# Loads, ones products and conditioning steps moved in a two-block transformer kernel

## What is computed

```
def first_block(x, ...):
    h = x
    for layer in range(DEPTH):                    # DEPTH = 2
        h = hybrid_layer(h, norm_gain[layer], w_in[layer], f_bias[layer], w_branch[layer], w_out[layer])
    return rms_norm(h, final_gain)

def modulate(x, g, shift, scale):
    return rms_norm_2(x, g) * (1 + scale) + shift

# second block, layer 0, for x and for ctx:
    h   = modulate(x,   norm1_g[0], sh1,  sc1)
    h_c = modulate(ctx, norm1_g[0], csh1, csc1)
    y, y_c = even_mixer(h, ...), even_mixer(h_c, ...)     # h @ w_in first: columns v, f, u
```

## Time and profile before

| | us |
|---|---|
| median of 3 runs | 1578.64 (1578.16 to 1579.22) |
| the profiled execution, whole | 1579.09 |
| its span on the core | 1577.3 |
| PE busy | 1538.7 |
| DVE busy | 1039.6 |
| ACT busy | 756.5 |

### The profile page before, as it was taken

How to read it: one execution, slowest core, us unless ns; L and a number is a source line. 1 busy time by engine, 2 the same in 40 slices (tenths; PEclk the granted TensorE clock), 3 DMA queues, 4 the chain that set the end, 5 groups by cost and what they waited for, 6 DMA issues and landing times.

```text
span 1577.3 us, 31432 instructions
## 1 busy us (share of the span) xinstructions
PE 1538.7 (98%) x13599; PEld 1472.3 (93%) x13599; DVE 1039.6 (66%) x1347; ACT 756.5 (48%) x1132; POOL 100.7 (6%) x79
## 2 busy tenths in 40 slices
PE   5999999999999999999999999999999999989999
PEld 5999999999999999899999999999999996889999
DVE  5878767578877775554456758886345347766674
ACT  4555554465465544653355322233245327655453
POOL 0311000003010000000020000000011002000000
PEclk9999999999999999999999999999999999989999
DMA  7676454566774546512035557754335224245854
GB/s 263 217 242 221 163 178 149 183 228 208 241 241 160 188 161 211 178 64 81 28 108 174 174 180 241 243 179 143 90 116 174 90 81 102 86 134 154 234 172 136
DMA packets 312333, 260.92 MB, mean 165 GB/s; under 512 B 24066, under 2 KB 298498, under 8 KB 312068
## 3 DMA queue, kind: packets, MB, share of 16 engines
q1 hardware_dynamic: 294260, 253.52, 49.6%
q10 hardware_dynamic: 17936, 5.40, 1.6%
HBM read 257.85 MB, written 1.05 MB: 164 GB/s over the span
## 4 chain that ended last, share of the span: by engine, by line
PE 54%; issue 7%; DVE 5%; ACT 3%; DMA 0%; POOL 0%; ACTq 0%; DVEq 0%; SPq 0%; POOLq 0%
PE banks_g L1417 34%; PE banks_g L967 7%; PE banks_g L1127 5%; PE banks_g L1276 2%; DVE w_lo L2498 1%; ACT near_p L2043 1%; DVE w_lo L2200 1%; PE banks_g L956 1%; ACT w_hi L1794 1%; PE banks_g L1378 1%; PE bank_s L1450 0%; POOL bias L2128 0%; PE bank_t L1464 0%; DVE near_max L2792 0%; PE bank_t L894 0%
## 5 line engine op out<-in xcount | busy, mean ns | idle before, releaser
L1417 PE MATMUL banks_g<-h_hi,w_lo 128*128 128x256 f32 x1296 | 360.5, 278 | 1.0 <-DVE w_lo L2498 0.6
L1417 PE MATMUL banks_g<-h_lo,w_hi 128*128 128x256 f32 x1296 | 358.5, 277 | 0.0
L1417 PE MATMUL banks_g<-h_hi,w_hi 128*128 128x256 f32 x1296 | 358.5, 277 | 0.0
L2498 DVE TENSOR_TENSOR w_lo<-raw,w_hi 128x2048 fp32r<-128x2048 f32 (+1 forms) x100 | 207.6, 2076 | 100.6 <-ACT w_hi L1794 100.3
L2200 DVE TENSOR_TENSOR w_lo<-raw,w_hi 128x2048 fp32r<-128x2048 f32 x92 | 212.4, 2310 | 72.5 <-ACT w_hi L1594 72.2
L1417 PEld LDWEIGHTS banks_g<-h_hi,w_lo 128*128 128x128 f32 x1296 | 243.5, 188 | 3.0 <-issue 0.9
L1417 PEld LDWEIGHTS banks_g<-h_hi,w_hi 128*128 128x128 f32 x1296 | 243.6, 188 | 0.0
L1417 PEld LDWEIGHTS banks_g<-h_lo,w_hi 128*128 128x128 f32 x1296 | 243.3, 188 | 0.1
L967 PE MATMUL banks_g<-h_hi,w_lo 128*128 128x256 f32 x800 | 226.0, 283 | 0.3 <-DVE w_lo L2200 0.3
L967 PE MATMUL banks_g<-h_hi,w_hi 128*128 128x256 f32 x800 | 221.4, 277 | 0.0
L967 PE MATMUL banks_g<-h_lo,w_hi 128*128 128x256 f32 x800 | 221.4, 277 | 0.0
(11 more groups left out here) (414 smaller groups left out, 3277.3 us busy)
## 6 DMA issues: line engine op xcount, KB each, us to landing
raw<-w_in SPq DMA_DIRECT2D x76, 1024.0 KB, 4.8
raw<-w_up SPq DMA_DIRECT2D x88, 512.0 KB, 4.9
ada_raw<-ada_w SPq DMA_DIRECT2D x24, 1024.0 KB, 7.1
raw<-w_down SPq DMA_DIRECT2D x32, 704.0 KB, 4.3
raw<-w_branch SPq DMA_DIRECT2D x12, 1024.0 KB, 4.9
ada_raw<-ada_t SPq DMA_DIRECT2D x12, 1024.0 KB, 4.9
late_raw<-ada_t SPq DMA_DIRECT2D x12, 1024.0 KB, 5.0
raw<-qkv SPq DMA_DIRECT2D x12, 1024.0 KB, 4.9
```

The source lines that it names most:

```text
L1417: last = nc.tensor.matmul(to, w[:, c, m0:m0 + P], a[:, c, s_ * SEQ:s_ * SEQ + SEQ], start=(m, s_, c, n) == (0, 0, 0, 0), stop=(m, s_, c, n ...
L2498: nc.vector.tensor_tensor(w_lo[:, u % SLOTS, 0:n], raw[:, u % SLOTS, 0:n], w_hi[:, u % SLOTS, 0:n].bitcast(F32), ALU.subtract).then_inc(dv ...
```

## The change

The parts, by place:

1. **Start.** `vectors` leads SP's queue and `ident` goes by ACT's; x follows in two halves of its columns, and the first weight unit in two halves of 512 KB; the loads of units 0 to 3 and of the first `ada_raw` no longer wait for PE. The six constant tables go behind unit 2 in SP's queue. PE multiplies a tile of ones by itself 8 times before the transposes and 12 times after them, into a bank that unit 0 overwrites. Unit 0 starts when the first half of its weights is split and asks for the second at chunk 4. DVE makes `o_lo` straight from the banks, and copies to `x_t` after that. The squares of x are summed along its rows by ACT (two `Square` with an accumulator), in place of four ACT squares, three DVE additions and four PE products; one small product keeps the step "sumsq" in PE's count.
2. **Between the layers.** ACT's splits of the next layer's first two units follow the squares of `out` 1 and 2, not 2 and 3.
3. **End of layer 1.** ctx comes in two transfers, issued at units 40 and 41, the first behind the products "values15"; four tables of the end go from there to the end's unit 2. The norm of ctx is made after units 39 and 41 to 43, its transposes follow units 43 and 44, its modulation units 44 and 45, its splits units 44, 45 and 47. The squares of x at the end of layer 1 get tiles of their own and are summed on DVE to two tiles, so that "final sums" is 8 products instead of 16; it stands inside the ctx part of `vs` 0 ahead of chunk 6, and "spread00" inside that of `vs` 1 ahead of chunk 4. The two x parts of `vs` are one loop over chunks, which feeds each chunk to both units.

```diff
+            order.append(("ctx prep", n - 40))
...
+        if n in (43, 44):
+            order += [("ctx turn", 2 * (n - 43)), ("ctx turn", 2 * (n - 43) + 1)]
+        if n in (44, 45):
+            order += [("ctx h", 4 * (n - 44) + c) for c in range(4)]
+        order.extend(("ctx split", b) for b, at in enumerate((44, 44, 45, 47)) if n == at)
...
+        if n == 39:
+            order.append(("ctx prep", 0))
+        if n == 41:
+            order.append(("ctx prep", 1))
...
-    order = [("ctx turn", b) for b in range(4)] + [("final sums",)]
...
+    order = [("final root",), ("second root",)]
...
-            sp.dma_start(ident[:, :], ins["ident"]).then_inc(x_loaded, 16)
-            sp.dma_start(vec_in, ins["vectors"].rearrange("(a p) f -> p a f", p=P)).then_inc(x_loaded, 16)
-            sp.dma_start(x_in, ins["x"][0].rearrange("(t p) f -> p t f", p=P)).then_inc(x_loaded, 16)
+            sp.dma_start(vec_in, ins["vectors"].rearrange("(a p) f -> p a f", p=P)).then_inc(vec_loaded, 16)
+            for n in range(2):
+                sp.dma_start(x_in[:, :, n * 512:n * 512 + 512],
+                             ins["x"][0].rearrange("(t p) f -> p t f", p=P)[:, :, n * 512:n * 512 + 512]
+                             ).then_inc(x_loaded[n], 16)
...
-                    sp.wait_ge(pe_steps, pe_.at(f"unit{before}", before=u < SLOTS))
-                    sp.sem_inc(sp_passed, 1)
+                    if layer or u >= SLOTS:
+                        sp.wait_ge(pe_steps, pe_.at(f"unit{before}", before=u < SLOTS))
+                        sp.sem_inc(sp_passed, 1)
...
+                    if (layer, u) == (0, 0):
+                        sp.dma_start(dst[:, 0:KC // 2, :], src[:, 0:KC // 2, :]).then_inc(half_loaded, 16)
+                        dst, src = dst[:, KC // 2:KC, :], src[:, KC // 2:KC, :]
                     sp.dma_start(dst, src).then_inc(raw_loaded[u % SLOTS], 16)
...
+                    if u in (40, 41) and layer == DEPTH - 1:
+                        t = u - 40
+                        if t == 0:
+                            sp.wait_ge(pe_steps, pe_.at("values15"))
+                        sp.dma_start(c_in[:, t, :], ins["ctx"][0, t * P:t * P + P, :]).then_inc(ctx_loaded[t], 16)
+                    if u == (1 if layer else 2):
...
+                        if layer == 0:
+                            for dst, src in ((rope[:, :, :], ins["rope"]), (causal[:, :, :], ins["causal"]),
+                                             (upto[:, :, :], ins["upto"]), (pick[:, :], ins["pick"]),
+                                             (add_parts[:, :], ins["add_parts"]),
+                                             (fbias[:, :, :].rearrange("p l h -> p (l h)"),
+                                              ins["forget_bias"].rearrange("(o l) h -> o (l h)", o=1
+                                                                           ).to_broadcast([P, DEPTH * 8]))):
+                                sp.dma_start(dst, src).then_inc(consts_loaded, 16)
...
+                        if u == (1 if (layer, n) == (0, 0) else min(slot_n + 2, len(UNITS) - 1)):
...
+                if u == 2:
+                    sp.dma_start(w_s[:, :, :], ins["w_s"].rearrange("g p q -> p g q")).then_inc(end_loaded, 16)
...
+                    sp.dma_start(dft_c[:, :], ins["dft_c"]).then_inc(end_loaded, 16)
+                    sp.dma_start(dft_t[:, :, :, :], ins["dft_t"]).then_inc(end_loaded, 16)
...
-            pe.wait_ge(x_loaded, 16 * 3)
+            def warm(n):
+                for _ in range(n):
+                    nc.tensor.matmul(bank_g[0][:, 0:P], ones[:, :], ones[:, :], start=True, stop=True)
+            pe.wait_ge(pool_steps, pool_.at("ones"))
+            warm(8)
+            pe.wait_ge(vec_loaded, 16 * 2)
...
+                if b % 2 == 0:
+                    pe.wait_ge(x_loaded[b // 2], 16)
...
+            warm(12)
...
+            def final_sums():
+                pe.wait_ge(x_squared, 9)
+                for n, parts in ((2, y_sq[:, 0, :, :]), (0, last_sq[:, 0:2, :])):
+                    for t in range(2):
+                        for j in range(2):
+                            mm = nc.tensor.matmul(bank_o[:, SUM_COL + n + t:SUM_COL + n + t + 1],
+                                                  parts[:, j, t * P:t * P + P], ones[:, 0:1],
+                                                  start=j == 0, stop=j == 1)
+                mm.then_inc(pe_steps, pe_.step("final sums"))
...
+                for c in range(KC):
+                    if i == 0 and c % 2 == 0:
+                        pe.wait_ge(ctx_split, c // 2 + 1)
+                    if (i, c) == (0, 6):
+                        final_sums()
+                    if (i, c) == (1, 4):
+                        spread00()
...
+            def vs_x():
+                ks = [END_JOBS[("vs", i, 0)] for i in range(2)]
+                pair = [tuple(halves(END_U[("vs", i)])) for i in range(2)]
+                for k in ks:
+                    bank_empty(k)
+                for c in range(KC):
+                    pe.wait_ge(dve_steps, dve_.at(f"x split{c}"))
+                    for i, (wh, wl) in enumerate(pair):
+                        for m in range(2):
+                            for n, (a, w) in enumerate(((h2_lo, wh), (h2_hi, wl), (h2_hi, wh))):
+                                last = nc.tensor.matmul(bank_g[ks[i] % BANKS][:, m * 256:m * 256 + 256],
+                                                        a[:, c, m * P:m * P + P], w[:, c, :],
+                                                        start=(m, c, n) == (0, 0, 0), stop=(m, c, n) == (1, KC - 1, 2))
+                        if c == KC - 1:
+                            last.then_inc(pe_steps, pe_.step(f"job{ks[i]}", f"unit{END_U[('vs', i)]}"))
...
+                if b % 2:
+                    n = b // 2
+                    act.wait_ge(raw_loaded[0] if n else half_loaded, 16)
+                    half = slice(n * UNIT // 2, (n + 1) * UNIT // 2)
+                    nc.scalar.activation(w_hi[:, 0, half], raw[:, 0, half], ACT.Copy
+                                         ).then_inc(act_steps, act_.step(f"first hi{n}"))
...
-            for i in range(4):
-                act.wait_ge(dve_start, i + 1)
-                squares(i)
+            act.wait_ge(raw_loaded[1], 16)
+            nc.scalar.activation(w_hi[:, 1, :], raw[:, 1, :], ACT.Copy).then_inc(act_steps, act_.step("hi1"))
...
+            for t in range(2):
+                nc.scalar.activation(qk[0][:, 4 * t:4 * t + 4, :].rearrange("p a t -> p (a t)"), x_in[:, t, :],
+                                     ACT.Square, accum_out=token_root1[:, t:t + 1]
+                                     ).then_inc(act_steps, act_.step("x rows"))
...
-                        if i >= 2:
-                            high(i - 2)
...
+                        if i in (1, 2):
+                            high(i - 1)
...
+            for c in range(KC):
+                if c % 2 == 0:
+                    dve.wait_ge(act_steps, act_.at(f"x hi{c + 1}"))
+                x_low(c, vec[:, n:n + KC], x_banks[c // 2][:, c % 2, :])
...
+                    nc.vector.tensor_tensor(w_lo[:, 0, half], raw[:, 0, half], w_hi[:, 0, half].bitcast(F32),
+                                            ALU.subtract).then_inc(first_lo if c // 4 else half_lo, 1)
...
+            for b in range(4):
+                nc.vector.tensor_copy(x_t[:, 2 * b:2 * b + 2, :], x_banks[b]).then_inc(dve_start, 1)
+                if b == 0:
+                    first_low(1)
...
+                        else:
+                            if i == 2:
+                                first_low(0)
+                            last_add(i, 1 + 2 * i)
                             nc.vector.tensor_tensor(y_sq[:, 0, :, :], y_sq[:, 0, :, :], y_sq[:, 1, :, :], ALU.add
                                                     ).then_inc(x_squared, 1)
+                            if i == 3:
+                                first_low(1)
...
+                    elif what == "ctx split" and layer == DEPTH - 1:
+                        b, = arg
+                        cs, t = slice(2 * b, 2 * b + 2), slice(SEQ, 2 * SEQ)
+                        dve.wait_ge(ctx_h, 2 * b + 2)
+                        nc.vector.tensor_copy(h2_hi[:, cs, t], h2[:, cs, t]).then_inc(ctx_high, 1)
+                        dve.wait_ge(ctx_high, b + 1)
+                        nc.vector.tensor_tensor(h2_lo[:, cs, t], h2[:, cs, t], h2_hi[:, cs, t].bitcast(F32),
+                                                ALU.subtract).then_inc(ctx_split, 1)
```

269 lines of the change are left out of this document (120 added, 149 removed).

## The result

The changed kernel took 1570.56 us (median of 4 runs, 1568.51 to 1572.28), the kernel before beside it 1578.93 (4 runs, 1578.16 to 1579.84): a ratio of 0.9946, 95% interval 0.9929 to 0.9963. It is faster, by 8.4 us where 16.5 were forecast, and outside the range of 1555 to 1569. The profiled run was the fastest of the four, 1568.51 us with a span of 1566.6, so its trace shows a saving of 10.7 us against 1577.3. One run of a later kernel (e12, 1915.78 us at a mean granted clock of 0.751) is of a slow state and is left out.

What follows compares the result with a forecast made beforehand. PE, busy 1538.7 of 1577.3 us, was taken as the bound. Gains of 10.2 (start), 0.6 (between layers) and 5.7 (end of layer 1, 7.9 - 2.2) made 16.5, so 1578.64 became 1562; range 1555 to 1569.

Steps and rivals of the forecast that it cites:

- the start: Opening up to the csum products: a gain of 10.2 us, decided by DVE's chain to `logf`; bounds 7 and 13.
- PE's start: PE's own path at the opening: unit 1's first product at 17.6 us, 13.0 us earlier than before.
- Landed at 23.9: Unit 3's load at the opening: 7.7 MB in all moved by 22.4 us, landed at 23.9 us.
- It must wait 2.6 us: Ahead of csum: PE arrives at 40.1 us and waits 2.6 us, with `logf` finished at 42.7.
- Rival (c): Opening: later landings, low clock and a longer DVE chain leave a gain of only 7 us; time 1565; chance 0.13.
- Between the layers: PE's 1.13 us wait for the next unit 0's split shrinks: gain 0.6 us, bounds 0 and 1.1.
- The context transposes: Sixteen ctx transposes moved ahead of unit 47: 2.2 us lost, including a 2.1 us PE wait for the second scaled copy.
- From unit 47 to `f` 0: End of layer 1: PE takes 28.8 us for 36.7, a gain of 7.9, with one new wait of 2.3 us.
- I take nothing: Clock price of two 2 us pauses, at 642.4 and before `f` 0: taken as nothing, between nothing and 2.4 us.
- Rival (b): End of layer 1 gives less: clock falls at one or both pauses, 2.4 us each; 1564.4 to 1566.8; chance 0.15.
- The table load: Moved ahead of unit 44's split: 1.28 us with no drain counted; a 1.38 us drain would make the sum 1.1 smaller.
- (e): Opening: loads don't start early, something else holds SP's queue; the gain is 2 or 3 us, time 1570; chance 0.07.

Runs made afterwards that it cites:

- e12: The changed kernel with 17 more products of ones between the x transposes and unit 0, holding unit 0 back: 1567.60 us, ratio 0.9931 to the kernel before.
- e6: The changed kernel without its 20 products of ones at the start: 1569.25 us, ratio 0.9940 to the kernel before.
- e9: The changed kernel with the loads of five small tables issued behind unit 3's load, not ahead of it: 1566.03 us, ratio 0.9918 to the kernel before.
- e1: The changed kernel with 18 more products of ones on PE ahead of its layer 0 wait for `logf`: 1566.42 us, ratio 0.9926 to the kernel before.
- e5: The changed kernel again with no edit, as base for other runs: 1570.09 us, ratio 0.9937 to the kernel before.
- e7: The changed kernel with the small turn, from which `logf` is made, ahead of the first piece of h, both layers: 1567.50 us, ratio 0.9924 to the kernel before.
- e2: The changed kernel with the csum products written one unit later, after unit 4, in both layers: 1567.24 us, ratio 0.9923 to the kernel before.

## Why the prediction was half right

The time fell outside the range, because the start gave 5.1 us and not 10.2. Two terms did that, the landing (1.9 us at csum) and the price of the wait (3.2).

- **PE's start** (13.0 us at unit 1): right, 12.9. It was also the term that mattered least (e12, e6).
- **"Landed at 23.9"**: 1.5 us too early. DMA was never idle for want of an issue (331 GB/s or more in every us from 5 to 30), so a sum of bytes was the right form. It had the rate 0.7 us too high and the landing 0.8 us too short: the 1.2 to 1.5 us from traffic to landing came from one transfer with nothing behind it. Cost: the 1.9 us by which csum missed 10.2 (8.3), 1.5 of them the landing. e9 shows this load to be on the chain.
- **"It must wait 2.6 us", priced as 2.6 us and nothing else**: the step that failed. I weighed the clock at the two pauses of the end and never asked it of this one, which I had made myself. It cost 3.2 us in the first trace (8.3 at csum to 5.1 behind unit 4), and e1 gives 3.0 back without touching the wait. Rival (c) had named a low clock at the start, but for the opening.
- **Between the layers 0.6**: 0.7; the wait of 1.13 is 0.28.
- **The context transposes, a loss of 2.2**: 2.1, with a wait of 2.04 where 2.1 was forecast.
- **From unit 47 to `f` 0, a gain of 7.9**: 7.4 (29.4 us for the 28.8 of the sum), with the wait of 2.38 where 2.3 was forecast.
- **"I take nothing" for the clock after pauses of 2 us**: wrong at `f` 0 in the first trace (1.6 us), right there in e5, right at `c_n` in the first trace, wrong in e7. Rival (b) was thus real but not certain: behind `c_n` the clock fell in five of ten traces, ahead of `f` 0 in five of nine. The Trainium skill (TensorE: Matmul & The Clock Gate, HAM oscillation) has only long pauses lower the clock; the wait of 2.38 us ahead of `f` 0 was followed by a granted clock of 0.53, so the trace decides against leaning on that for pauses of this size.
- **The table load**: it takes 1.28 us and the next step starts 0.01 us behind it (40.91, 42.20). The drain that the Trainium skill (ScalarE: Activation LUTs, What ACT_TABLE_LOAD costs) adds is not in these rows.

Two of the prediction's own signs came: unit 3 landed behind 25 us, its sign of being wrong, and the granted clock fell below 0.9, its sign of (b).

In the profiled span: 5.1 + 0.7 - 2.1 + 7.4 - 1.6 = 9.5 us at the turn of `w_s`, and 10.7 at the end. The last 1.2 us come late, and no run here tells why. Both kernels have a stretch of low clock between 1370 and 1400 us, and it differs from trace to trace (0.77 in the first trace's 1370 to 1380, 0.66 in e5's), so it may be that. **Rival (c)**, a start worth 7 us, came nearest in its mechanism, though by the time alone the 1570 of (e) is nearer, whose mechanism failed, since the loads did start early. But (c) came near for half of another reason: of its three causes only the late landing was there, and the low clock stood behind the wait and not in the opening. The other 2 us between 10.6 (1579.09 less 1568.51, the two profiled runs) and 8.4 in the medians are the three slower runs of the four, which left no trace. Their clock was 0.992 to 0.994 beside 0.995, as it would be if the clock fell once or twice more; that is argued, not shown.

## What to carry to other kernels

When a bottleneck engine is brought forward past what feeds it, price the new wait twice: its length, and the clock behind it. Then ask which chain ends that wait and work on that one; here a swap of two steps took the whole wait away (e7). A lead won early can be capped again at another engine's next deadline (near 70 us in e7 and e2), so look for that before adding gains up. And when a load's landing is summed from the bytes ahead of it, allow for those issued right behind it: here 0.9 MB of them moved before it landed, 0.8 us later than summed.
